# Two-layer hybrid trunk on one core: expert outputs placed back inside the next pair, gate folded into the hidden product, first norm and pool scale fed differently

## The chip, the cores and the metric
The kernel runs on one core of one Trainium2 chip. The metric is the device time of one execution in microseconds, as a median of several runs. The core has TensorE (PE in the profile), VectorE (DVE), ScalarE (ACT), GpSimd (POOL) and SyncE (SP); sixteen DMA engines fill its on-chip memory from HBM. PE writes its products to PSUM (eight banks of 512 fp32 columns on 128 partitions), from where DVE and ACT read them.

## What is computed
256 tokens of 2048 features go through two layers. Layer 0 mixes tokens by a causal trailing mean in four feature groups, layer 1 by stick-breaking attention on keys and values made from the stream; each is followed by a mixture of 16 experts, of which every token takes two of one group of four. The sizes: D = 2048, expert width F = 512.

```python
def pool_mixer(x, pool_w, pool_scale):          # four groups of 512 features, windows 2, 4, 8, 16
    ...
    y = jnp.einsum("bsgc,gcd->bsgd", pooled, pool_w).reshape(B, S, D)
    return y * pool_scale

def hier_moe(x, w_grp, b_grp, w_rt, b_rt, w_gate, w_up, w_down):
    ...                                          # gate: (T, 16), two entries of a row are not zero
    h = jax.nn.silu(jnp.einsum("td,edf->tef", xt, w_gate)) * jnp.einsum("td,edf->tef", xt, w_up)
    y = jnp.einsum("tef,efd->td", h * gate[:, :, None], w_down)
    return y.reshape(B, S, D)

def reference(...):
    for i in range(2):
        if i == 0: h = h + pool_mixer(rmsnorm(h, norm_mix[0]), ...)
        else:      h = h + stick_breaking_layer(rmsnorm(h, norm_mix[1]), k, v, ...)
        h = h + hier_moe(rmsnorm(h, norm_ffn[i]), ...)
```

## The kernel before
**Weights.** They are read once, in loads of 1 MiB issued by SP into a ring of 12 slots (`ring`). An expert takes 12 slots: four of gate and four of up, in turn (`m` = 0 to 7), and four of down (`m` = 8 to 11). A load into a slot waits until PE has read what is there (`slot_read`, L378 in the loop, L341 before it), so a wait of PE can hold back loads. The first five loads of expert 1 go to a buffer of their own (`extra`, L362).

**Experts.** `moe(l)` on each engine does the router and then 16 experts in 8 pairs; on PE pair 0 stands outside a hardware loop over the other seven. At most 64 tokens (CAP) of an expert are handled; a branch for more stands behind the loops and isn't taken here. For each expert `e` of a pair (`b` = 0, 1), PE does:
- gate and up (L1308): 32 fp32 products of `xg` (the gathered tokens, transposed) with four quarters of the weights; the gate half goes to partitions 0 to 63, the up half to 64 to 127. After each quarter two slots are free.
- the gather of the next expert (L1258 for its three parts of the norm factor `rs`, L1264 for 16 feature tiles, 96 small bf16 products with the 0/1 matrix `pick`)
- transposes: of `put`, 0/1 times the gate (L1318), and of `hid` (L1320)
- down (L1331): 16 fp32 products of `hidT` with the down weights, a slot free after each four.

ACT makes silu of the gate half with the scale `rs_slot` (L542) once all eight slots are read; DVE multiplies it with the up half to `hid` (L918); ACT copies `putT` and `hidT` (L545, L546), and PE waits for these ahead of down. ACT and DVE copy the outputs of down to `y_rows` (L551, L928), two quarters each. After both experts of a pair PE puts the rows back to their tokens: eight fp32 products of `putT` (128 x 256) with `y_rows` (L1341), each into a bank that DVE adds to the stream `resid` (L938); a product waits for the add but one before it.

**Router.** Ahead of the loop PE makes the logits, DVE picks the groups and experts in some 30 small steps (L815 to L894), PE counts slots, and `gather(0)` collects the tokens of expert 0. PE runs products of constants in between (`keep_clock`, L1229). DVE then scales the gathered tokens to `xg` (L904), first half and second half; the first gate product waits for the first half.

**Opening and pooling.** x and the band table are loaded by ACT's queue, the constants and norm vectors by SP's. PE transposes the vectors (L1387), DVE spreads them and makes the first norm (L801; POOL does the power, L449) and the scaled bands (L976); PE's band products (L1397, L1398) follow, ACT and DVE split them into two fp32r parts (L580, L983). The four groups of the pooling product run as units of 12 fp32r products (L1179), weights split by ACT (L501) and DVE (L764). The pool scale, a row in `vec_rows`, is spread over the partitions by PE (L1222, bank 7), copied by ACT to `mixed` (L589), multiplied on DVE with the product (L1003) and added to `resid` (L1007). The router's parts of the stream follow group by group on ACT, POOL (L456, L462) and DVE (L777, L783).

## Time and profile before

| | us |
|---|---|
| three runs | 1464.21, 1467.04, 1467.81 |
| median | 1467.04 |
| the profiled execution | 1467.67, of which the span from first to last instruction is 1465.8 |
| PE busy in the span | 1386.4 |
| expert loop of layer 0 on PE | about 87.9 to 555.8 |
| expert loop of layer 1 on PE | about 992.3 to 1461.5 |

The page gives busy time by engine; a view by windows gives for a stretch the busy time of each engine with the number of its instructions, the granted clock of PE (1.00 is 2.4 GHz, 0.50 is 1.2 GHz), the busy share of the DMA engines and what they moved; the timeline merges like instructions that follow each other (start, length, what, how many), with the idle time ahead of them and what ended it in brackets. PE shows two records for one fp32 product. Numbers with L are lines of the kernel.

### The profile page before, as it was taken

The page shows a single profiled execution, that of the slowest core. Times are in us where ns is not written, and L with a number is a line of the kernel's source. Part 1 is how long each engine was busy: PE and PEld are TensorE (multiplying, and loading weights), DVE is VectorE, ACT ScalarE, POOL GpSimd, SP SyncE. Part 2 cuts the span into 40 slices and gives each one's busy share as a digit, 9 for nine tenths or more (in the row PEclk, how much of TensorE's full clock was granted, in tenths as well). Part 3 has the DMA queues.
Part 4 walks back from the last instruction along what each step waited for, and adds up shares of the span by engine and source line. Part 5 has one row for each costly group of instructions (what it writes and reads, how often), then busy time and mean ns, then how long its engine had stood idle before and what let it go on. Part 6 is the DMA issues. An engine that isn't in the chain of part 4 may idle for free.

```text
span 1465.8 us, 22517 instructions
## 1 busy us (share of the span) xinstructions
PE 1386.4 (95%) x9100; PEld 767.0 (52%) x9100; DVE 530.1 (36%) x832; ACT 387.2 (26%) x585; POOL 40.3 (3%) x33
## 2 busy tenths in 40 slices
PE   6889999999999998999999998989999999999998
PEld 5653334334333436888888887764343343333433
DVE  3742121221221215656566665561213212212122
ACT  3621011000010115565656565440001001100010
POOL 0110000000000000100000000010000000000000
PEclk9989999999999998999999999999999999999999
DMA  9768899999999999554554543568799999999995
GB/s 327 323 253 351 363 422 422 422 422 422 422 422 422 422 411 326 173 181 164 162 175 150 172 156 132 176 248 337 291 422 421 422 422 421 422 422 422 422 422 231
DMA packets 95028, 480.62 MB, mean 328 GB/s; under 512 B 9218, under 2 KB 9316, under 8 KB 45572
## 3 DMA queue, kind: packets, MB, share of 16 engines
q1 hardware_dynamic: 94548, 477.07, 82.1%
q10 hardware_dynamic: 432, 2.88, 0.5%
q8 instruction: 34, 0.56, 0.1%
q14 instruction: 14, 0.11, 0.0%
HBM read 477.82 MB, written 2.10 MB: 327 GB/s over the span
## 4 chain that ended last, share of the span: by engine, by line
issue 53%; PE 39%; DVE 3%; ACT 3%; POOL 1%; DMA 1%; SPq 0%; POOLq 0%; ACTq 0%; DVEq 0%
PE ps L1308 15%; PE ps L1331 8%; PE ps L1179 6%; PE ps L1341 4%; PE ps L1264 3%; POOL head_rs L485 1%; DVE ws L764 1%; ACT parts L517 1%; DMA vec_rows<-in_q_norm 1%; ACT ws L501 1%; PE ps L1397 1%; PE ps L1320 0%; DVE rest L777 0%; ACT hidT L546 0%; ACT junk L514 0%
## 5 line engine op out<-in xcount | busy, mean ns | idle before, releaser
L1308 PE MATMUL ps<-ring,xg 128*64 128x512 f32 x1968 | 432.0, 593 | 0.6 <-issue 0.6
L1179 PE MATMUL ps<-ws,xs 128*128 128x512 f32 x1632 | 385.4, 395 | 7.0 <-DVE ws L764 2.8
L1179 PEld LDWEIGHTS ps<-ws,xs 128*128 128x128 f32 x1632 | 304.9, 189 | 75.5 <-DVE ws L764 5.3
L1308 PEld LDWEIGHTS ps<-ring,xg 128*64 128x64 f32 x1968 | 142.8, 137 | 279.2 <-issue 279.2
L1331 PE MATMUL ps<-ring,hidT 128*64 128x512 f32 x1024 | 226.8, 595 | 21.9 <-ACT hidT L546 21.9
L918 DVE SCALAR_TENSOR_TENSOR hid<-ps,rs_slot,silu_g 64x512 f32<-64x512 f32 x32 | 24.0, 752 | 433.0 <-ACT silu_g L542 433.0
L767 DVE SCALAR_TENSOR_TENSOR ws<-ring,vecs,ws 128x512 fp32r<-128x512 f32 x192 | 134.5, 748 | 92.0 <-ACT ws L504 92.0
L542 ACT ACTIVATE silu_g<-ps,rs_slot 64x512 f32<-64x512 f32 x32 | 21.8, 682 | 514.4 <-PE ps L1308 514.4
L1331 PEld LDWEIGHTS ps<-ring,hidT 128*64 128x64 f32 x1024 | 73.8, 137 | 151.2 <-issue 131.7
L504 ACT ACTIVATE ws<-ring,vecs 128x512 fp32r<-128x512 f32 x192 | 127.4, 715 | 94.2 <-PE ps L1179 86.1
L1341 PE MATMUL ps<-y_rows,putT 128*128 128x512 f32 x256 | 123.4, 618 | 12.1 <-ACT y_rows L551 12.0
L928 DVE COPY y_rows<-ps 64x512 f32<-64x512 f32 x64 | 41.6, 690 | 238.5 <-PE ps L1331 238.5
L1264 PE MATMUL ps<-pick,parts 128*128 128x64 bf16 x3264 | 102.2, 194 | 0.0
L938 DVE TENSOR_TENSOR resid<-resid,ps 128x512 f32<-128x512 f32 x128 | 87.9, 687 | 30.4 <-PE ps L1341 28.6
L1264 PEld LDWEIGHTS ps<-pick,parts 128*128 128x128 bf16 x3264 | 98.2, 98 | 0.5
L551 ACT ACTIVATE y_rows<-ps 64x512 f32<-64x512 f32 x64 | 34.3, 584 | 231.3 <-PE ps L1331 231.3
L1341 PEld LDWEIGHTS ps<-y_rows,putT 128*128 128x128 f32 x256 | 39.8, 188 | 96.6 <-DVE resid L938 58.0
L764 DVE TENSOR_TENSOR ws<-ring,ws 128x1024 fp32r<-128x1024 f32 x40 | 50.5, 1267 | 51.9 <-ACT ws L501 51.9
L904 DVE TENSOR_TENSOR xg<-ps,ffn_gain 128x512 f32<-128x512 f32 x68 | 46.4, 682 | 24.0 <-PE ps L1264 24.0
L501 ACT ACTIVATE ws<-ring 128x1024 fp32r<-128x1024 f32 x40 | 41.5, 1053 | 46.6 <-PE ps L1179 38.8
L545 ACT ACTIVATE putT<-ps 128x128 f32<-128x128 f32 x32 | 8.9, 277 | 88.7 <-PE ps L1320 88.7
L485 POOL TENSOR_TENSOR head_rs<-head_ssq,half 128x8 f32<-128x8 f32 x8 | 16.7, 2082 | 251.1 <-DVE head_ssq L1029 251.1
(153 smaller groups left out, 640.2 us busy)
## 6 DMA issues: line engine op xcount, KB each, us to landing
ring<-in_moe_w_down SPq DMA_DIRECT2D x128, 1024.0 KB, 15.5
ring<-in_moe_w_up SPq DMA_DIRECT2D x124, 1024.0 KB, 15.0
ring<-in_moe_w_gate SPq DMA_DIRECT2D x122, 1024.0 KB, 13.2
ring<-in_w_kv SPq DMA_DIRECT2D x32, 1024.0 KB, 5.5
ring<-in_w_q SPq DMA_DIRECT2D x16, 1024.0 KB, 5.0
ring<-in_w_o SPq DMA_DIRECT2D x16, 1024.0 KB, 5.0
extra<-in_moe_w_gate SPq DMA_DIRECT2D x6, 1024.0 KB, 7.8
ring<-in_pool_w SPq DMA_DIRECT2D x4, 1024.0 KB, 15.4
```

Source lines behind the costliest of these rows:

```text
L501: nc.scalar.activation(dst, four(n)[:, 2 * h:2 * h + 2, :], ACT.Copy).then_inc(unit_hi, 1)
L504: last = nc.scalar.activation(dst[:, k, :], four(n)[:, 2 * h + k, :], ACT.Copy, scale=vecs[:, gain + k:gain + k + 1])
L764: nc.vector.tensor_tensor(ws[:, b, 1], src, ws[:, b, 0].bitcast(F32), ALU.subtract).then_inc(unit_lo, 1)
L767: last = nc.vector.scalar_tensor_tensor(out=ws[:, b, 1, k, :], in0=src[:, k, :], scalar=vecs[:, gain + k:gain + k + 1], in1=ws[:, b, 0, k, ...
L904: nc.vector.tensor_tensor(xg[:, b, 8 * h:8 * h + 8, :], ps[:, 6 + h, :].rearrange("p (k s) -> p k s", k=8), per_feature(ffn_gain[:, l, 8 * ...
L928: nc.vector.tensor_copy(y_rows[CAP * b:CAP * b + CAP, (2 * h + 1) * BLK:(2 * h + 2) * BLK], ps[CAP:2 * CAP, 2 + h, :]).then_inc(y_dve, 1)
L938: nc.vector.tensor_tensor(rb, rb, ps[:, 4 + t, :], ALU.add).then_inc(resid_added, 1)
L1179: last = mm(ps[:, bank + t, :], xs[:, px, k, cols], ws[:, b, pw, j, :], start=(first and j == 0 and n == 0), stop=(last_unit and j == 1 an ...
L1264: last = mm(ps[:, 6 + k // 8, (k % 8) * CAP:(k % 8 + 1) * CAP], parts[:, s, t, k * P:(k + 1) * P], pick[:, t, e, :], start=(s == 0 and t = ...
L1308: last = mm(ps[CAP * h:CAP * h + CAP, b, :], xg[:, b, k, :], both[h][:, j, :], start=(k == 0), stop=(k == KD - 1))
L1331: last = mm(ps[CAP * h:CAP * h + CAP, 2 + c // 2, :], hidT[:, b, k, :], down[:, c * BLK:(c + 1) * BLK], start=(k == 0), stop=(k == KF - 1))
L1341: mm(ps[:, 4 + t, :], putT[:, t * P:(t + 1) * P], y_rows[:, c * BLK:(c + 1) * BLK], start=True, stop=True).then_inc(mix_done, 1)
```

## The change
**Experts.** The gate is no longer in the matrix that puts the rows back but in the silu-up product: `gate` times `rs` is split into three bf16 parts (`gate_parts`, five DVE steps ahead of the loop), which are gathered with those of `rs` in one product of six columns (`side`, `make_side`); DVE sums both (`slot_scale`), ACT uses the first for silu, DVE the second for `hid`. `put` and its making go; PE makes `putT` from `pick` itself, by two bf16 products with the identity, once per pair. The outputs of down are taken by ACT alone, rounded to fp32r (`y_hi`), and DVE subtracts that from the output in PSUM to get the rest (`y_lo`, eight operations a pair). Putting back is 16 fp32r products a pair, and they stand in the next pair, two outputs after each quarter of its first gate and up step; those of the last pair stand behind the loop. DVE's adds of a pair move to the head of the next pair, ahead of `hid`. The gather is split: 11 of 16 tiles stand ahead of the transposes, the rest behind them, ahead of the wait for `hidT`. For expert 0 the scales are gathered after the tokens, not before.

**Opening and pooling.** The constants are loaded after the norm vectors; the pool scale is spread by DMA with broadcast (groups 0 and 1 by SP ahead of the router's rows and the second pooling weight, groups 2 and 3 by POOL once the buffer's former rows are used) to `scale_row`; PE's spreading and ACT's copies go. DVE multiplies the product in PSUM in place and adds from there; PE may use the bank again after the add, not after the multiplication. The first mean square stands ahead of DVE's wait for the transposed vectors. PE's products of constants at the start number 56 pairs of 128 columns instead of 9 of 256, need only a memset, and stand ahead of the wait for the tables; those of the router (24 and 10) have the same columns as before, in halves.

```diff
+gate_parts = at(26 * KB + 512, "gate_parts", [P, NT, EXP + 2, 3], BF16)
...
+y_lo012 = at(96 * KB, "y_lo012", [P, 3, BLK], F32R)
+y_lo = [y_lo012[:, 0, :], y_lo012[:, 1, :], y_lo012[:, 2, :], y_lo3[:, :]]
 member = at(27 * KB + 512, "member", [P, NT, EXP], BF16)
...
-WARM_START, WARM_ROUTE, WARM_PICK = 9, 24, 10
+WARM_START, WARM_ROUTE, WARM_PICK = 56, 24, 10
+TURN_AT = 11
...
-    sp.dma_start(const[:], table).then_inc(table_loaded, 16)
...
     sp.dma_start(vec_rows[V_HEAD + 1:V_END, :], q_norm).then_inc(band_loaded, 16)
-    sp.dma_start(vec_rows[V_SCALE:V_ROWS, :], pool_scale.rearrange("a (k p) -> (a k) p", p=P)).then_inc(table_loaded, 16)
+    sp.dma_start(const[:], table).then_inc(table_loaded, 16)
     load(0, pool_w_v[0])
...
+    for g in range(2):
+        sp.dma_start(scale_row[:, g, :], pool_scale[:, g * BLK:(g + 1) * BLK].to_broadcast([P, BLK])).then_inc(scale_loaded[g], 16)
...
+    for g in range(2, NG):
+        pool.wait_ge(mixed_done, 2 * (g - 2) + 2)
+        pool.dma_start(scale_row[:, g % 2, :], pool_scale[:, g * BLK:(g + 1) * BLK].to_broadcast([P, BLK])).then_inc(scale_loaded[g], 16)
...
                 act.wait_ge(slot_read, n0 + SLOTS * (2 * i + b) + 8)
                 nc.scalar.activation(silu_g[:, :], ps[0:CAP, b, :], ACT.Silu,
-                                     scale=rs_slot[:, b:b + 1]).then_inc(silu_done, 1)
+                                     scale=slot_scale[:, b, 0:1]).then_inc(silu_done, 1)
                 act.wait_ge(hid_turned, EXP * l + 2 * i + b + 1)
-                nc.scalar.activation(putT[:, b * P:(b + 1) * P], ps[:, 1 - b, SEQ:SEQ + P], ACT.Copy)
                 nc.scalar.activation(hidT[:, b], ps[:, 1 - b, 0:KF * CAP].rearrange("p (k s) -> p k s", k=KF),
                                      ACT.Copy).then_inc(hidT_done, 1)
+                if b == 0:
+                    nc.scalar.activation(putT[:, :], ps[:, 1, SEQ:2 * SEQ], ACT.Copy).then_inc(putT_done, 1)
...
+                for c in range(NBLK):
+                    h = c % 2
+                    nc.scalar.activation(y_hi[CAP * b:CAP * b + CAP, c, :],
+                                         ps[CAP * h:CAP * h + CAP, 2 + c // 2, :],
+                                         ACT.Copy).then_inc(y_hi_done, 1)
...
-        act.wait_ge(scale_spread, g + 1)
-        if g:
-            act.wait_ge(resid_added, 2 * g)
-        nc.scalar.activation(mixed[:, :, :], ps[:, 7, :].unsqueeze(1).to_broadcast([P, NT, BLK]),
-                             ACT.Copy).then_inc(scale_out, 1)
...
+        step(nc.vector.tensor_tensor(rs_parts[:, :, 2], rs_rest[:, :], rs_parts[:, :, 1], ALU.subtract))
+        nc.vector.tensor_copy(side[:, :, 0, 0:3], rs_parts[:, :, :])
+        nc.vector.tensor_copy(side[:, :, 1, 0:3], rs_parts[:, :, :])
...
-        def make_put(i):
-            dve.wait_ge(pick_done, (NPAIR + 1) * l + i + 1)
-            nc.vector.tensor_tensor(put[:, :, :, :], pick[:, :, :, :],
-                                    gate[:, :, bass.ds(2 * i, 2)].unsqueeze(3).to_broadcast([P, NT, 2, CAP]),
-                                    ALU.mult).then_inc(put_done, 1)
+        def make_side(i):
+            nc.vector.tensor_copy(side[:, :, :, 3:6], gate_parts[:, :, bass.ds(2 * i, 2), :]).then_inc(side_done, 1)
...
+        step(nc.vector.tensor_tensor(gate_rs[:, :, :], gate[:, :, 0:EXP],
+                                     rs[:, :].unsqueeze(2).to_broadcast([P, NT, EXP]), ALU.mult))
+        step(nc.vector.tensor_copy(gate_parts[:, :, 0:EXP, 0], gate_rs[:, :, :]))
+        step(nc.vector.tensor_tensor(gate_rest[:, :, :], gate_rs[:, :, :], gate_parts[:, :, 0:EXP, 0], ALU.subtract))
+        step(nc.vector.tensor_copy(gate_parts[:, :, 0:EXP, 1], gate_rest[:, :, :]))
+        step(nc.vector.tensor_tensor(gate_parts[:, :, 0:EXP, 2], gate_rest[:, :, :], gate_parts[:, :, 0:EXP, 1],
+                                     ALU.subtract))
+        make_side(0)
...
         tokens_out(G0 + 1, 0)
-        make_put(0)
...
-            dve.wait_ge(hid_turned, EXP * l + 2 * i + 2)
-            make_put(i + 1)
...
+        def add_rows(i):
             for m in range(8):
                 c, t = m // 2, m % 2
                 dve.wait_ge(mix_done, 8 * NPAIR * l + 8 * i + m + 1)
                 rb = resid[:, t, c * BLK:(c + 1) * BLK]
                 nc.vector.tensor_tensor(rb, rb, ps[:, 4 + t, :], ALU.add).then_inc(resid_added, 1)
+        def pair(i, before=None):
+            if before is not None:
+                add_rows(before)
+            for b in range(2):
+                dve.wait_ge(silu_done, EXP * l + 2 * i + b + 1)
+                nc.vector.scalar_tensor_tensor(out=hid[:, :], in0=ps[CAP:2 * CAP, b, :],
+                                               scalar=slot_scale[:, b, 1:2], in1=silu_g[:, :],
+                                               op0=ALU.mult, op1=ALU.mult).then_inc(hid_done, 1)
+                tokens_out(G0 + 2 * i + 2 + b, 1 - b)
+                if b == 0:
+                    dve.wait_ge(hid_turned, EXP * l + 2 * i + 1)
+                    make_pick(i + 1)
+                    make_side(i + 1)
+                for c in range(NBLK):
+                    h = c % 2
+                    dve.wait_ge(y_hi_done, NBLK * (EXP * l + 2 * i + b) + c + 1)
+                    nc.vector.tensor_tensor(y_lo[c][CAP * b:CAP * b + CAP, :], ps[CAP * h:CAP * h + CAP, 2 + c // 2, :],
+                                            y_hi[CAP * b:CAP * b + CAP, c, :].bitcast(F32),
+                                            ALU.subtract).then_inc(y_lo_done, 1)
+        pair(0)
+        with dve.Fori(1, NPAIR) as i:
+            pair(i, i - 1)
+        add_rows(NPAIR - 1)
...
+    nc.vector.memset(counters[:, 1, :], 1.0).then_inc(ones_done, 1)
+    mean_square(0, True)
     dve.wait_ge(vec_turned, 1)
...
     nc.vector.tensor_copy(counters[:, 0, :], tri)
-    nc.vector.tensor_copy(ident_b[:, :], ident)
-    nc.vector.tensor_copy(counters[:, 1, :], ones).then_inc(vec_done, 1)
-    mean_square(0, True)
+    nc.vector.tensor_copy(ident_b[:, :], ident).then_inc(vec_done, 1)
...
-                dve.wait_ge(scale_out, g + 1)
+                dve.wait_ge(scale_loaded[g], 16)
...
-            nc.vector.tensor_tensor(mixed[:, t, :], ps[:, MIX_BANKS[g % 2] + t, :], mixed[:, t, :],
-                                    ALU.mult).then_inc(mixed_done, 1)
+            mixed = ps[:, MIX_BANKS[g % 2] + t, :]
+            nc.vector.tensor_tensor(mixed, mixed, scale_row[:, g % 2, :], ALU.mult).then_inc(mixed_done, 1)
             rb = resid[:, t, g * BLK:(g + 1) * BLK]
             dve.wait_ge(mixed_done, 2 * g + t + 1)
-            nc.vector.tensor_tensor(rb, rb, mixed[:, t, :], ALU.add).then_inc(resid_added, 1)
+            nc.vector.tensor_tensor(rb, rb, mixed, ALU.add).then_inc(resid_added, 1)
...
-    def spread_scale(g):
-        if g:
-            pe.wait_ge(scale_out, g)
-        for k in range(4):
-            row = V_SCALE + 4 * g + k
-            last = mm(ps[:, 7, k * P:(k + 1) * P], const[0:V_ROWS, row:row + 1].to_broadcast([V_ROWS, P]),
...
-        last.then_inc(scale_spread, 1)
...
-            mm(ps[:, 3, 0:2 * P], counters[:, 0, :], counters[:, :, :].rearrange("p a b -> p (a b)"),
-               start=True, stop=True)
+            for c in (0, P):
+                mm(ps[:, 3, c:c + P], counters[:, 1, :], counters[:, 1, :], start=True, stop=True)
...
-                last = mm(ps[0:CAP, e, 508:511], pick[:, t, e, :], rs_parts[:, t, :], start=(t == 0),
+                last = mm(ps[0:CAP, e, 506:512], pick[:, t, e, :], side[:, t, e, :], start=(t == 0),
                           stop=(t == NT - 1))
...
+        def gather(e, tiles):
+            for k in tiles:
...
-        pe.wait_ge(rs_parts_done, l + 1)
         pe.wait_ge(pick_done, PICKS + 1)
-        gather(0)
+        gather(0, range(KD))
+        pe.wait_ge(side_done, PICKS + 1)
+        gather_scales(0)
...
+        def put_rows(i, m):
...
+            c, t = m // 2, m % 2
+            if t == 0:
+                pe.wait_ge(y_lo_done, NBLK * (EXP * l + 2 * i + 1) + c + 1)
+            pe.wait_ge(resid_added, add0 + 8 * i + m - 1)
+            mm(ps[:, 4 + t, :], putT[:, t * P:(t + 1) * P], y_hi[:, c, :], start=True, stop=False)
+            mm(ps[:, 4 + t, :], putT[:, t * P:(t + 1) * P], y_lo[c], start=False, stop=True).then_inc(mix_done, 1)
+        def pair(i, before=None):
             for b in range(2):
                 pe.wait_ge(xg_done, 2 * (XG + 2 * i + b) + 1)
                 pe.wait_ge(hidT_done, (EXP + 1) * l + 2 * i + b + 1)
+                if b == 1:
+                    pe.wait_ge(putT_done, NPAIR * l + i + 1)
                 for q in range(4):
                     both = [loaded(i, b, 2 * q + h).rearrange("p (k c) -> p k c", k=4) for h in range(2)]
                     if q == 2:
...
                     last.then_inc(slot_read, 2)
+                    if b == 0 and before is not None:
+                        put_rows(before, 2 * q)
+                        put_rows(before, 2 * q + 1)
...
-                pe.wait_ge(rs_slot_done, XG + 2 * i + b + 2)
-                pe.wait_ge(put_done, PICKS + i + 1)
+                    pe.wait_ge(side_done, PICKS + i + 2)
+                gather_scales(1 - b)
+                gather(1 - b, range(TURN_AT))
+                pe.wait_ge(slot_scale_done, XG + 2 * i + b + 2)
                 pe.wait_ge(hid_done, EXP * l + 2 * i + b + 1)
-                nc.tensor.transpose(ps[:, 1 - b, SEQ:SEQ + P], put[:, b].rearrange("p e s -> p (e s)"), ident)
+                if b == 0:
+                    for t in range(NT):
+                        mm(ps[:, 1, SEQ + t * P:SEQ + (t + 1) * P], pick[:, t].rearrange("p e s -> p (e s)"),
+                           ident_b[:, :], start=True, stop=True)
+                else:
+                    gather(0, range(TURN_AT, TURN_AT + 1))
                 for k in range(KF):
                     last = nc.tensor.transpose(ps[:, 1 - b, k * CAP:(k + 1) * CAP], hid[:, k * P:(k + 1) * P],
                                                const[0:CAP, C_ID:C_ID + CAP])
                 last.then_inc(hid_turned, 1)
+                gather(1 - b, range(TURN_AT + b, KD))
                 pe.wait_ge(hidT_done, (EXP + 1) * l + 2 * i + b + 2)
                 if b == 1:
-                    pe.wait_ge(y_act, 2 * (EXP * l + 2 * i) + 2)
-                    pe.wait_ge(y_dve, 2 * (EXP * l + 2 * i) + 2)
+                    pe.wait_ge(y_lo_done, NBLK * (EXP * l + 2 * i + 1))
...
-            for m in range(8):
-                c, t = m // 2, m % 2
-                if t == 0:
-                    pe.wait_ge((y_act, y_dve)[c % 2], 2 * (EXP * l + 2 * i) + 3 + c // 2)
-                pe.wait_ge(resid_added, add0 + 8 * i + m - 1)
-                mm(ps[:, 4 + t, :], putT[:, t * P:(t + 1) * P], y_rows[:, c * BLK:(c + 1) * BLK],
-                   start=True, stop=True).then_inc(mix_done, 1)
...
         pair(0)
         with pe.Fori(1, NPAIR) as i:
-            pair(i)
+            pair(i, i - 1)
+        for m in range(8):
+            put_rows(NPAIR - 1, m)
...
+    pe.wait_ge(ones_done, 1)
+    keep_clock(WARM_START)
     pe.wait_ge(table_loaded, TABLES)
     pe.wait_ge(band_loaded, 32)
     nc.tensor.transpose(ps[:, 4, 0:V_END], vec_rows[0:V_END, :], const[0:V_END, C_ID:C_ID + V_END]).then_inc(vec_turned, 1)
-    pe.wait_ge(vec_done, 1)
-    keep_clock(WARM_START)
...
-                pe.wait_ge(mixed_done, 2 * (g - 2) + t + 1)
+                pe.wait_ge(resid_added, 2 * (g - 2) + t + 1)
         unit(2 * g, (4 * g, 4 * g + 1), True, False, read, bank=MIX_BANKS[g % 2])
-        spread_scale(g)
         unit(2 * g + 1, (4 * g + 2, 4 * g + 3), False, True, bank=MIX_BANKS[g % 2])
```

## Rows read from the trace of the kernel before

**Rows 1.** The page: busy time, share of the span, instructions of each engine
```profile
PE 1386.4 (95%) x9100; PEld 767.0 (52%) x9100; DVE 530.1 (36%) x832; ACT 387.2 (26%) x585; POOL 40.3 (3%) x33
```

**Rows 2.** View by windows: one pair of experts in layer 0 (columns above)
```profile
199.68:258.34 58.66, 56.61 (x416) 22.93 (x414) 13.42 (x23) 5.89 (x11) 0.00 (x0) 1.00 1.01 422
```

**Rows 3.** Timeline of PE: one pair of layer 0, and the start of the next
```profile
204.87 13.95 PE L1308 MATMUL ps<-ring,xg 128*64 128x512 f32 x64
...
218.79 2.97 PE L1264 MATMUL ps<-pick,parts 128*128 128x64 bf16 x96
221.60 0.31 PE L1318 MATMUL ps<-const,put 128*128 128x128 f32 x1
...
222.94 7.09 PE L1331 MATMUL ps<-ring,hidT 128*64 128x512 f32 x32 [0.64 <-ACT hidT L546]
...
255.72 7.70 PE L1341 MATMUL ps<-y_rows,putT 128*128 128x512 f32 x16 [0.77 <-ACT y_rows L551]
263.34 1.94 PE L1308 MATMUL ps<-ring,xg 128*64 128x512 f32 x8
```

**Rows 4.** Tile ring: landing times, loads issued 208.6 to 267.0, then 442.5 to 500.9
```profile
DMA to landing us min/median/max: 7.3/13.5/18.8
...
DMA to landing us min/median/max: 12.1/18.3/23.6
```

**Rows 5.** PE timeline and ring landings: expert 15 of layer 0, then of layer 1
```profile
522.19 13.90 PE L1308 MATMUL ps<-ring,xg 128*64 128x512 f32 x64
...
L378 SPq DMA_DIRECT2D ring<-in_moe_w_up x1: 333/333/333, 511.8 to 511.8; - x1
...
DMA to landing us min/median/max: 19.9/19.9/19.9
...
1427.80 13.90 PE L1308 MATMUL ps<-ring,xg 128*64 128x512 f32 x64
...
L378 SPq DMA_DIRECT2D ring<-in_moe_w_up x1: 333/333/333, 1417.5 to 1417.5; - x1
...
DMA to landing us min/median/max: 18.8/18.8/18.8
```

**Rows 6.** View by windows: pair 0 and the start of pair 1
```profile
120.00:160.00 40.00, 38.63 (x247) 14.96 (x244) 9.41 (x15) 3.59 (x6) 0.00 (x0) 1.00 0.79 302
```

**Rows 7.** Chain by time: 48 fp32r products; the page's group of DVE's adds
```profile
857.12 10.91 PE ps L1179 x48
...
L938 DVE TENSOR_TENSOR resid<-resid,ps 128x512 f32<-128x512 f32 x128 | 87.9, 687 | 30.4 <-PE ps L1341 28.6
```

**Rows 8.** Tile ring: two loads issued one after the other, and their landings
```profile
L341 SPq DMA_DIRECT2D ring<-in_moe_w_down x1: 328/328/328, 137.9 to 137.9; - x1
...
DMA to landing us min/median/max: 8.0/8.0/8.0
...
L341 SPq DMA_DIRECT2D ring<-in_moe_w_gate x1: 327/327/327, 150.1 to 150.1; - x1
...
DMA to landing us min/median/max: 4.7/4.7/4.7
```

**Rows 9.** Timeline: the gates of layer 0 are made, and the first expert product
```profile
85.88 0.18 DVE L894 TENSOR_TENSOR gate<-route 128x32 f32<-128x32 f32 x1
...
87.85 5.37 PE L1308 MATMUL ps<-ring,xg 128*64 128x512 f32 x24 [0.41 <-issue]
```

**Rows 10.** Timeline of the pooling stage: a spread scale on PE, DVE in group 3
```profile
44.38 1.05 PE L1222 MATMUL ps<-vec_rows,const 98*128 98x128 f32 x8
...
66.40 0.69 DVE L1003 TENSOR_TENSOR mixed<-ps,mixed 128x512 f32<-128x512 f32 x1 [0.74 <-ACT mixed L589]
```

**Rows 11.** Timeline of the opening: the scaled bands, and the first pooling unit
```profile
15.04 1.15 DVE L976 TENSOR_SCALAR band_s<-band,rs 128x1024 f32<-128x1024 f32 x2 [0.89 <-POOL rs L449]
...
32.56 5.49 PE L1179 MATMUL ps<-ws,xs 128*128 128x512 f32 x12
```

**Rows 12.** View by windows: PE waits for DVE ahead of the router
```profile
65.00:75.00 10.00, 3.21 (x20) 1.98 (x24) 8.46 (x13) 7.51 (x15) 3.69 (x3) 0.70 0.74 306
```

73 lines of the change are left out of this document (25 added, 48 removed).

## The prediction, made before the changed kernel was run

> **What bounds the kernel now.** I read the page first, then the stretches of the expert loops, then the landings of the weight loads. The page says 95% busy for PE [rows 1], which invites the conclusion that every matmul removed is time gained. The view by windows corrects it: over one pair of experts PE is busy 56.6 of 58.66 us, but in the same stretch the DMA engines are at 1.01 of their share and move 422 GB/s [rows 2]. A pair of experts needs 24 loads of 1 MiB, 25.17 MB, and 25.17 MB at 422 GB/s is 59.6 us. PE takes a pair in 58.47 us (from the first matmul of one pair at 204.87 to that of the next at 263.34 [rows 3]). So PE already consumes faster than the queue delivers, and lives on a lead. The landings show that lead melting: the shortest time from issue to landing within a pair is 7.3 us for the pair issued from 208.7 and 12.1 us four pairs later [rows 4], 1.2 us more in each pair; 58.47 + 1.2 = 59.67 us, the same number by another road. One load therefore lands every 2.486 us (59.67 / 24). No matmul of the loop waits for a load in this trace, but the lead is nearly used up when a layer ends. In the last pair of layer 0 the last up block of expert 15 is issued at 511.8 and lands 19.9 us later, at 531.7; PE started that expert at 522.19 and came to that block (last quarter of 13.8 us) at 532.5. The lead is 0.8 us. In layer 1 the same block lands at 1417.5 + 18.8 = 1436.3, and PE came to it at 1427.80 + 10.3 = 1438.1, 1.8 us of lead [rows 5].
>
> What remains to be gained in a layer is then: the lead, the time in which the queue stood idle before it became continuous, and what follows the last load. The queue stood idle around pair 0: 302 GB/s over 120 to 160 us is 302/422, so 11.4 us of 40 were lost; after that it never stops [rows 2, 6].
>
> **The change part by part: the loop.** Of the 58.47 us [rows 3]: the eight fp32 put products and the wait for ACT in front of them, from 254.95 (255.72 less 0.77) to 263.34, are 8.39. They become 16 fp32r products. 48 fp32r products of the same 128x512 shape took 10.91 us, 0.227 each [rows 7], so 16 cost 3.64. Two waits of 0.64 for hidT go: the left-over gather tiles (5 of 16, a fraction of the 2.81 us from 218.79 to 221.60, so 0.9 us) cover the copy, and if that cover fails each expert pays the 0.64 again. The two fp32 transposes of put (0.3 each) become two bf16 products, some 0.12 together by the pace of the gather. PE's new need per pair: 58.47 - 8.39 + 3.64 - 1.28 - 0.6 + 0.12 = 52.0 us. New waits: the put products stand on PE between the quarters of the next gate and up step and wait for y_lo and for the adds; behind them stand the next quarter and, through it, the freeing of slots. The first is due 3.4 us after the pair before ends, y_lo of that block is ready after about 1.4 us (an ACT copy and one subtraction), each next one 0.7 later, and one quarter brings DVE only two adds, so none of these waits bites. DVE loses four copies and gains eight subtractions of some 0.69 [rows 7] a pair, 13.4 to about 16 of 59 us [rows 2]; that is hidden. The order on DVE (adds of the old pair first, then hid) could hold the transposes by under 1 us; hidden as well, as follows.
>
> 52.0 us is under the 59.67 us that the queue needs. **From pair 1 on the loop becomes DMA-bound**, with PE waiting some 7.7 us a pair for loads, in pieces of at most about 1.5 us (a quarter of the gate and up step takes 3.44 us and its two loads arrive in 4.97). So almost all of the 6.5 us saved in a pair is not gained. What is gained is worked out for each layer.
>
> *The gap of the queue.* The last down load of expert 2 is issued at 137.9 and lands 8.0 us later, at 145.9; the next one (expert 3) waits until the first quarter of pair 1 has been read, issue 150.1, landing 4.7 us later, at 154.8 [rows 8]. Between the two issues lie the 8.39 us of the put. With the put gone from there, and the two experts of pair 0 shorter by some 0.9 us each, that issue comes at about 140, and its landing is limited by the one before it: that one was late too and comes at about 143.6, so 143.6 + 2.5 = 146.1. Gain 8.7 us of the 11.4. From there each load is 2.486 us behind the one before, to the end of the layer, so the last load moves by the same 8.7 us. The same gap stands in layer 1.
> *After the last gate and up load.* PE now reaches it exactly when it lands: the lead of 0.8 us (layer 0) and 1.8 us (layer 1) is gained. Then the hidT wait and the put transpose are gone: 0.9 us.
> *The tail of a layer.* The last pair's put has no next pair to hide in. After the last down product ACT copies (0.6), DVE subtracts four times and then adds eight times, 12 x 0.69 = 8.3 us on one engine [rows 7]; before, 8.39 + 0.69. I take 0.4 us gained.
>
> **The router stage in front of each loop.** gather(0) moves ahead and now ends before its scales, while DVE must make five more steps (gate times rs, and its three parts) after the gates at 85.88, and copy them, before the scales can be gathered, reduced and xg scaled. One such step is 0.2 us. Gates at 86.1 plus 0.35 (two more copies and one more wait before slot_of) plus 5 x 0.2 plus 0.2 gives 87.7; scales 0.2, reduction 0.25, first half of xg 0.7, so PE starts at 88.9 instead of 87.85 [rows 9]. Cost 1.1 us in each layer, and it is fully paid, since the queue is waiting for PE to free slots there.
>
> **Pooling stage.** The four spreads of the pool scale (eight PE records each, 1.05 us [rows 10]) and ACT's four copies of them go; the product is made in PSUM, at the same DVE price. Two of the spreads lie on the chain that leads PE, ACT, DVE to the mixed rows of group 1: twice 1.05 less a little overlap with the units' products, 1.75 us. In group 3 DVE also waited 0.74 us for ACT's copy [rows 10]. Together 2.5 us. The two loads that POOL issues instead wait for the mixed rows of groups 0 and 1 and stand ahead of its first subtraction, for which DVE and ACT have other work; their data are due two groups later, some 10 us. No row shows a DMA issued by POOL; the bounds are nothing, and two of POOL's mean operations (40.3/33 = 1.2 us [rows 1]), 2.4 us, if none of it is covered. POOL is 3% busy, so I take nothing.
>
> **Opening.** DVE's first norm no longer stands behind the vector copies: POOL's inverse root, for which DVE waited 0.89 us before 15.04, comes earlier; band_s is ready about 1.1 us sooner [rows 11]. Against it: 0.5 MB of broadcast scale now lies ahead of the second pool_w load (1.2 us at 422 GB/s, up to double for short rows), on which ACT's copies and so the xs parts depend, and PE, warmed before the vectors arrive, then idles until band_s is there, so that the first band products may run at 1.2 GHz (a unit of 12 products took 5.49 us at that level against 2.75 [rows 11]). No row shows how these mix; bounds -1 (gain) to +3, I take +0.7.
>
> **Sum** against the profiled execution (span 1465.8, time 1467.67): opening and pooling +0.7 - 2.5 = -1.8. Layer 0: +1.1 - 8.7 - 0.8 - 0.9 - 0.4 = -9.7. Layer 1: +1.1 - 8.7 - 1.8 - 0.9 - 0.4 = -10.7. Total -22.2, so 1445.5 us; this run stands 0.6 us above the median of the three, 1467.04, so **1445 us**.
>
> A page of the Trainium skill, "DMA: Bandwidth & Descriptors" (section Specifications), names a ceiling of 435 GB/s for the core's 16 DMA engines, 3% over what this queue does. By that rule a load would land every 2.41 us, and the sum, an estimate from that page, would come to about 1422 us. The trace does not show it: with landings 12 to 24 us after their issue [rows 4], so a full queue, the rate stays at 422 [rows 2]. The same section gives 358 GB/s as the limit of HBM per core; this trace is 18% above that, so the measurement decides.
>
> **Rivals.** (1) *The queue has speed in reserve.* The rate seen is then only what PE asked for. For it: PE never waits for a load now. Against it: the time to landing grows from pair to pair, which a queue with reserve would not show [rows 4]. If it were so, PE's 52.0 us a pair would set the time at the far end: some 41 us a layer, 1467 - 83 - 1 = about 1383 us. Short of that, about 155 loads a layer follow the gap, so each percent of reserve is 155 x 0.025 = 3.9 us a layer; 3% give 1422 us. Chance 0.05 for all of it. The ceiling that the page names would be this rival's case of 3%. (2) *The gap is not refilled*, because something else holds the first loads of pair 1: then only leads, transposes, tails, pooling remain, 22.2 - 17.4 = 4.8, so 1462 us. Chance 0.05. (3) *The opening costs its upper bound*: +2.3 on my value, and POOL's 2.4, so 1450 us. Chance 0.10. (4) *Slower: the clock falls in the loop.* PE now waits in every quarter. In this trace the granted clock fell after PE had done nothing from 65 to 70 us, and 65 to 75 shows 0.70 on average [rows 12]. A stretch of s us at 1.2 GHz costs PE s/2. PE has 7.7 us a pair to spare and the change 22 us over 15 pairs to lose, so it turns slower from (7.7 + 1.5) x 2 = 18 us at 1.2 GHz in each pair. At 25 us in each pair: (12.5 - 7.7) x 15 = 72, so 1445 + 72 = 1517 us. Against it: the longest new wait is 1.5 us, and the loops now, with waits of 0.8 us, are granted 1.00 throughout [rows 2]. Chance 0.04.
>
> **How the numbers follow.** My forecast has 0.72, its own range 1440 to 1450 (the bounds of the opening and of POOL, and 0.2% for the rate, worth 1 us per layer); the rivals 0.05, 0.05, 0.10, 0.04; 0.04 is left for what I do not see. The range of 8 in 10 takes in the forecast and rival 3: 1438 to 1453. A measurement of this kernel tells about 0.3% (4.4 us) from no change, so faster is below 1462.6: 0.91 (forecast, rivals 1 and 3, half of 2, and part of the rest), same 0.05, slower 0.04.
>
> **What would show it right or wrong.** In the loop of the changed kernel: a period of 59.6 to 59.7 us, longer than now; 422 GB/s; PE waits ahead of the gate and up products, released by loads of ring, some 7 us a pair; the wait ahead of the down products gone. The window 120 to 160 near 400 GB/s. The first expert product about 0.7 us earlier in layer 0. It is wrong if the period follows PE's 52 us, if the clock shows 0.5 in the loops, or if a new wait ahead of the transposes exceeds what the loads leave.

## The result and the profile after

The changed kernel takes **1447.94 us** (median of 4 runs, 1446.9 to 1450.29) against 1465.96 us of the kernel before beside it: ratio 0.988, 95% interval 0.986 to 0.990. The forecast was 1445. The profiled run is the longest of the four: 1450.29 us, span 1448.4, against 1467.67 and 1465.8; the step by step account below is between these two, 17.4 us.

View by windows of the changed kernel (columns as in [rows 2]): a pair in which PE still has loads in hand, a pair in which it has none, pair 0 to 1, and two stretches that are discussed below.
```profile
203.60:263.30 59.70, 59.70 (x481) 26.06 (x481) 18.13 (x31) 9.10 (x15) 0.00 (x0) 1.00 1.01 422
382.60:442.30 59.70, 54.70 (x424) 23.51 (x419) 15.46 (x26) 8.47 (x15) 0.00 (x0) 1.00 1.01 422
120.00:160.00 40.00, 40.00 (x354) 18.32 (x350) 12.71 (x22) 6.05 (x10) 0.00 (x0) 1.00 0.96 389
541.00:547.50 6.50, 5.39 (x11) 3.27 (x12) 4.30 (x8) 0.00 (x0) 0.00 (x0) 0.50 1.05 386
886.00:889.00 3.00, 3.00 (x8) 2.33 (x8) 0.71 (x1) 0.00 (x0) 0.00 (x0) 0.50 0.03 10
```
The queue runs at the same 422 GB/s as before [rows 2]. What changed is at its two ends: 389 instead of 302 GB/s around pair 0 [rows 6], that is 3.1 instead of 11.4 us of 40 lost, and later in the layer PE waits for loads. The page's busy times (to set against [rows 1]), its group of gate and up products, and the landing times of the loads issued from 442.5 to 501 (to set against [rows 4]):
```profile
PE 1358.4 (94%) x9239; PEld 775.5 (54%) x9239; DVE 567.1 (39%) x910; ACT 423.4 (29%) x629; POOL 41.3 (3%) x35
...
L1337 PE MATMUL ps<-ring,xg 128*64 128x512 f32 x1968 | 447.1, 596 | 45.4 <-DMA ring<-in_moe_w_up 43.0
...
DMA to landing us min/median/max: 21.8/23.7/25.5
```
Timeline of PE: two starts of a pair with loads in hand and the last down step between them, the first wait for a load, an expert later in the layer, then the last expert of layer 0 (compare [rows 3, 5]).
```profile
189.49 3.60 PE L1337 MATMUL ps<-ring,xg 128*64 128x512 f32 x16
...
236.13 7.09 PE L1369 MATMUL ps<-ring,hidT 128*64 128x512 f32 x32
...
243.04 3.60 PE L1337 MATMUL ps<-ring,xg 128*64 128x512 f32 x16
...
280.14 3.65 PE L1337 MATMUL ps<-ring,xg 128*64 128x512 f32 x16 [0.66 <-DMA ring<-in_moe_w_up]
...
449.40 3.60 PE L1337 MATMUL ps<-ring,xg 128*64 128x512 f32 x16
453.99 3.65 PE L1337 MATMUL ps<-ring,xg 128*64 128x512 f32 x16 [0.99 <-DMA ring<-in_moe_w_up]
459.06 3.65 PE L1337 MATMUL ps<-ring,xg 128*64 128x512 f32 x16 [1.42 <-DMA ring<-in_moe_w_up]
463.94 3.65 PE L1337 MATMUL ps<-ring,xg 128*64 128x512 f32 x16 [1.22 <-DMA ring<-in_moe_w_up]
...
523.61 3.65 PE L1337 MATMUL ps<-ring,xg 128*64 128x512 f32 x16 [1.22 <-DMA ring<-in_moe_w_up]
...
530.60 7.09 PE L1369 MATMUL ps<-ring,hidT 128*64 128x512 f32 x32
```
PE's own pace is 243.04 - 189.49 = 53.55 us a pair; the queue's is 59.67 (the load that lands at 147.7 and the one that lands at 523.4 are 151 loads apart, 2.49 us for each). PE catches up with the queue at 280, in pair 3, and from there waits in every step of gate and up, down to the last: the last up load of layer 0 lands at 523.4 and PE goes on at 523.61.

The same points in both profiled runs, in us from the start. The third column is the shift so far, the fourth what this step adds, the fifth what the prediction had for it.

| point | before | after | shift | step | predicted |
|---|---|---|---|---|---|
| first extra load issued (end of pooling) | 63.53 | 61.94 | -1.6 | -1.6 | -1.8 |
| first expert product, layer 0 | 87.85 | 87.36 | -0.5 | +1.1 | +1.1 |
| last up load lands | 531.7 | 523.4 | -8.3 | -7.8 | -8.7 |
| last down step begins | 540.20 | 530.60 | -9.6 | -1.3 | -1.7 |
| last add ends | 556.47 | 548.78 | -7.7 | +1.9 | -0.4 |
| first attention product | 569.61 | 559.01 | -10.6 | -2.9 | 0 |
| first load freed at layer 1's router | 902.10 | 892.61 | -9.5 | +1.1 | 0 |
| first load freed by layer 1's experts | 999.81 | 991.21 | -8.6 | +0.9 | +1.1 |
| last up load lands | 1436.3 | 1419.6 | -16.7 | -8.1 | -8.7 |
| last down step begins | 1446.01 | 1426.67 | -19.3 | -2.6 | -2.7 |
| last add ends | 1462.27 | 1444.14 | -18.1 | +1.2 | -0.4 |
| end of the span | 1465.8 | 1448.4 | -17.4 | +0.7 | 0 |

Each column is one execution, and some of these steps differ by 1 to 3 us between executions of the same code; where the other profiles show that, it is said below.

### The profile page after: what moved, and what is told of

Its sections match the earlier page's. It is cut to its first block, busy times and chain, and to the rows that moved or that the text cites. A ratio compares the mean times of both kernels' runs of the same rounds, so it can differ in the third digit from the quotient of the medians.

```text
span 1448.4 us, 22975 instructions
## 1 busy us (share of the span) xinstructions
PE 1358.4 (94%) x9239; PEld 775.5 (54%) x9239; DVE 567.1 (39%) x910; ACT 423.4 (29%) x629; POOL 41.3 (3%) x35
## 4 chain that ended last, share of the span: by engine, by line
issue 53%; PE 24%; DMA 16%; DVE 3%; ACT 2%; POOL 1%; SPq 0%; POOLq 0%; DVEq 0%; ACTq 0%
DMA ring<-in_moe_w_up 16%; PE ps L1337 9%; PE ps L1204 6%; PE ps L1369 3%; PE ps L1281 2%; POOL head_rs L496 1%; PE ps L1319 1%; DVE ws L772 1%; DMA const<-in_constant_table 1%; PE ps L1428 1%; ACT parts L528 1%; ACT ws L512 1%; PE ps L1320 1%; DVE rest L785 0%; ACT junk L525 0%
## 5 line engine op out<-in xcount | busy, mean ns | idle before, releaser
L1337 PE MATMUL ps<-ring,xg 128*64 128x512 f32 x1968 | 447.1, 596 | 45.4 <-DMA ring<-in_moe_w_up 43.0
L956 DVE TENSOR_TENSOR y_lo<-ps,y_hi 64x512 fp32r<-64x512 f32 x128 | 88.2, 689 | 218.9 <-ACT y_hi L564 215.9
L553 ACT ACTIVATE silu_g<-ps,slot_scale 64x512 f32<-64x512 f32 x32 | 21.8, 683 | 460.7 <-PE ps L1337 460.7
L564 ACT ACTIVATE y_hi<-ps 64x512 fp32r<-64x512 f32 x128 | 75.7, 591 | 239.2 <-PE ps L1369 236.8
L944 DVE SCALAR_TENSOR_TENSOR hid<-ps,slot_scale,silu_g 64x512 f32<-64x512 f32 x32 | 24.1, 752 | 242.8 <-ACT silu_g L553 242.4
L1281 PE MATMUL ps<-pick,parts 128*128 128x64 bf16 x3264 | 107.8, 194 | 0.8 <-DVE pick L878 0.8
L1319 PE MATMUL ps<-y_hi,putT 128*128 128x512 f32 x128 | 59.6, 465 | 6.5 <-DVE resid L936 3.5
L1319 PEld LDWEIGHTS ps<-y_hi,putT 128*128 128x128 f32 x128 | 24.9, 195 | 61.4 <-issue 48.2
L1320 PE MATMUL ps<-y_lo,putT 128*128 128x512 f32 x128 | 52.7, 412 | 0.0
L556 ACT ACTIVATE hidT<-ps 128x256 f32<-128x256 f32 x32 | 12.3, 384 | 78.3 <-PE ps L1358 78.3
```

Of the source, the lines that this page charges most:

```text
L564: nc.scalar.activation(y_hi[CAP * b:CAP * b + CAP, c, :], ps[CAP * h:CAP * h + CAP, 2 + c // 2, :], ACT.Copy).then_inc(y_hi_done, 1)
L956: nc.vector.tensor_tensor(y_lo[c][CAP * b:CAP * b + CAP, :], ps[CAP * h:CAP * h + CAP, 2 + c // 2, :], y_hi[CAP * b:CAP * b + CAP, c, :].b ...
L1281: last = mm(ps[:, 6 + k // 8, (k % 8) * CAP:(k % 8 + 1) * CAP], parts[:, s, t, k * P:(k + 1) * P], pick[:, t, e, :], start=(s == 0 and t = ...
L1319: mm(ps[:, 4 + t, :], putT[:, t * P:(t + 1) * P], y_hi[:, c, :], start=True, stop=False)
L1320: mm(ps[:, 4 + t, :], putT[:, t * P:(t + 1) * P], y_lo[c], start=False, stop=True).then_inc(mix_done, 1)
L1337: last = mm(ps[CAP * h:CAP * h + CAP, b, :], xg[:, b, k, :], both[h][:, j, :], start=(k == 0), stop=(k == KD - 1))
```

## The experiments

**Was it the queue's gap?** First the part that has nothing to do with the experts is taken back, then the place of the put.

*e1: old opening and pooling.* The edit takes back every part of the change ahead of the router:
```
-            pe.wait_ge(ones_done, 1)
-            keep_clock(WARM_START)
             pe.wait_ge(table_loaded, TABLES)
...
+            pe.wait_ge(vec_done, 1)
+            keep_clock(WARM_START)
...
                 unit(2 * g, (4 * g, 4 * g + 1), True, False, read, bank=MIX_BANKS[g % 2])
+                spread_scale(g)
```


> The changed kernel with its opening and pooling part put back as it was before the change (order of the first norm, spread of the pool scale by PE and ACT, nine warming products behind the vectors); the experts' part stays new. Theory: opening and pooling brought the 1.6 us by which the extra loads at the end of pooling are issued earlier in the changed kernel, and what is gained there is kept to the end: 1447.9 + 1.6 = 1449.5 us. Rival: that gain is lost again later (the half-clock stretch of 3.4 us at the end of the attention stage, which only the changed kernel has, comes from it): 1447.9 or a little less, and that stretch is gone.

Measured: 1453.1 us, ratio 0.991 (0.989 to 0.993). That is 3.6 us over the expectation. In its profile the first extra load is issued at 63.7 us, 1.8 later than in the profiled run of the changed kernel, and the span is 2.8 longer. But that run is at the edge here: in nine profiles with the changed kernel's opening and pooling (its own, that of e12, which is the same kernel again, and those of the versions e2 to e6, e8 and e9 below, which leave this part as it is) the load is issued between 59.6 and 61.9 us, 60.7 in the middle one; with the old part it is 63.5, 63.7 and 63.7 (the kernel before, e7, which is a version of it, and e1). First the changed kernel as profiled, then e3:
```profile
L369 SPq DMA_DIRECT2D extra<-in_moe_w_gate x3: 327/431/433, 61.9 to 74.8; - x3
...
L369 SPq DMA_DIRECT2D extra<-in_moe_w_gate x3: 328/432/433, 59.6 to 72.5; - x3
```
So opening and pooling bring 1.6 to 4.1 us at their own place, 3.0 in the middle. All four runs of this kernel (1451.5 to 1453.7) are slower than all four of the changed one, by 5.2 us in the medians; where the other 2 us go isn't shown. The rival falls: the half-clock stretch near 886 is there too, from 890 on.

*e2: the put at the end of its own pair.*
```
-                            if b == 0 and before is not None:
-                                put_rows(before, 2 * q)
-                                put_rows(before, 2 * q + 1)
...
                             last.then_inc(slot_read, 1)
+                    for m in range(8):
+                        put_rows(i, m)
```


> The changed kernel, but the put products of a pair stand at its own end again (still two fp32r passes), and so do the adds. PE then waits 1.4 us for the first y_lo and is held by DVE's four subtractions and eight adds: some 8.2 us between the last down product of a pair and the next pair's first product, instead of 4.5 us of put inside the next pair. PE's pair is 53.55 - 4.5 + 8.2 = 57.3 us, below the queue's 59.67. Theory (what was gained is the gap of the queue at pair 0 and 1): the gap comes back, 7.7 to 8.2 us in each layer, 1447.9 + 16 = 1464 us, within 3. Rival (the fp32r put gave the gain by being short on PE, wherever it stands): 1448 to 1450. Second rival (PE's pace counts, 3.7 us more in each of 16 pairs): 1448 + 60 = 1508.

Measured: 1464.4 us, ratio 0.9985 (0.9975 to 0.9994): nearly everything that the change brought is gone. Windows and timeline of this kernel:
```profile
120.00:160.00 40.00, 36.65 (x305) 16.79 (x301) 11.60 (x19) 5.39 (x8) 0.00 (x0) 0.96 0.79 309
...
203.60:263.30 59.70, 56.41 (x424) 24.59 (x422) 15.56 (x26) 8.42 (x14) 0.00 (x0) 0.97 1.01 422
...
529.08 3.65 PE L1335 MATMUL ps<-ring,xg 128*64 128x512 f32 x16 [1.09 <-DMA ring<-in_moe_w_up]
```
309 GB/s around pair 0, as before the change, and the last quarter of expert 15 still waits 1.09 us for its load: the queue sets the end of the layer, and the queue is late by its gap. Halving the put's passes brought nothing where it stood; from the last down product of a pair to the next pair's first product it takes 9.5 us (250.07 to 259.59), or 8.8 in a pair that keeps the full clock (192.63 to 201.38), against 8.4 before [rows 3]. At the end of six of layer 0's eight pairs the granted clock falls to 0.50 for some us, after PE stood still twice for 1.4 to 1.8 us; at the end of the other two it stays at 1.00 after waits of 1.5 and 1.6 us; this is the only kernel here in which rival 4, a fall within the loop, is seen.

**How much does PE have to spare?** The prediction said 7.7 us in each pair. Products were added to PE behind the down step of the first expert of pairs 1 to 7 (n of them, 8 in e3 and 24 in e4):
```
+                            if b == 0 and k == KF - 1 and before is not None:
+                                pe.wait_ge(resid_added, add0 + 8 * before + 8)
+                                for _ in range(n):
+                                    last = mm(ps[0:CAP, 4, :], hidT[:, b, k, :], down[:, 0:BLK], start=True, stop=True)
```


> The changed kernel with 8 more fp32 products of 128x512 behind the down step of the first expert of pairs 1 to 7 (written to a bank that is free then, used by nobody). A product of this shape takes 13.9/64 = 0.217 us, so PE gets 1.74 us more in a pair, 12.2 us in a layer. PE waited for loads 43.0 us in the two layers of the changed kernel, 21.5 us in each. Theory (account of a layer: nothing is lost until the added work is over 21.5 us): 1447.9 to 1449.5. Rival (PE sets the time): + 14 x 1.74 = 24 us, 1472.

> The same with 24 products: 5.2 us more in a pair, PE's pair 58.8 us, still under the 59.67 us of the queue; 36.5 us in a layer. Account of a layer: 36.5 - 21.5 = 15 us lost in each, 1448 + 30 = 1478, within 5, since PE begins pair 1 behind the queue and must catch up with it. Account by the pair, as the prediction had it (7.7 us to spare in each pair, every pair for itself): 1448 to 1450. PE sets the time from the first product on: + 73, 1521.

Measured: 1488.2 us (+40.2) and 1681.7 us (+233.8). All expectations missed, since the added products cost four times what I had put down for them. Starts of pairs in the kernel with 8, then in that with 24, and 24 added products in a row (each leaves two records; one is missing):
```profile
314.94 3.60 PE L1337 MATMUL ps<-ring,xg 128*64 128x512 f32 x16
...
375.36 3.60 PE L1337 MATMUL ps<-ring,xg 128*64 128x512 f32 x16
...
283.48 3.60 PE L1337 MATMUL ps<-ring,xg 128*64 128x512 f32 x16
...
312.89 20.33 PE L1374 MATMUL ps<-ring,hidT 128*64 128x512 f32 x47
...
357.67 3.60 PE L1337 MATMUL ps<-ring,xg 128*64 128x512 f32 x16
```
A pair takes 60.42 and 74.19 us instead of 53.55: 6.87 and 20.64 more, 0.86 for each product. With the right price the two runs decide after all. By the pair, 60.42 is only 0.75 over the queue's 59.67, so 14 pairs should lose 10.5 us; 40.2 were lost. By the layer, 7 x 6.87 = 48.1 us were added and 20.1 lost, and 144.5 added and 116.9 lost: 28.0 and 27.6 us were free. The timeline of the changed kernel gives nearly that: at its own pace PE would have begun the last down step at 236.13 + 5 x 53.55 = 503.9 us, and it began at 530.60, 26.7 us later. (The 43.0 us of the page, 21.5 a layer, are less; the starts count the wait in full, while the idle time is taken from a matmul's modelled end.) So PE has 28/7 = 4.0 us a pair to spare, not 7.7: in pairs 1 and 2 it is not waiting but catching up.

*e5: 4 products.* The account of the layer is put to a test that it could fail:

> The changed kernel with 4 added fp32 products behind the down step of the first expert of pairs 1 to 7. Alone in its place such a product took 0.86 us in the runs with 8 and 24 of them (PE's pair 60.42 and 74.19 us against 53.55 unhindered), not the 0.217 us that I had divided out of a step in which products for two halves of the array run side by side. So 3.44 us a pair, 24.1 us in a layer; PE's pair 57.0 us. Account of a layer, mended by those two runs (they lost 40.2 and 233.8 us for 96.2 and 289 us of added work, so about 28 us of a layer are free, which is 6.12 us of waiting in each of the last 4.65 pairs): 24.1 is under 28, so 1447.9 to 1449.5 us. Rival (PE's pace sets the time): + 48, 1496.

Measured: 1450.5 us (1449.2 to 1453.5), ratio 0.990 (0.988 to 0.992). PE got 48 us more to do, and the time rose by some 2, 1 more than the account had at most and far from the rival's 1496; the waits for loads shrink from 43.0 to 5.1 us on the page:
```profile
L1337 PE MATMUL ps<-ring,xg 128*64 128x512 f32 x1968 | 453.3, 595 | 7.3 <-DMA ring<-in_moe_w_up 5.1
```

**Who sets the pace, before and after?** The down loads are made half as large, in both kernels (e6 the changed one, e7 the one before). The down products read the loaded half twice, so the second half of the down result is left out:
```
-                return w_down_v[l, e, :, m - 8, :]
+                return w_down_v[l, e, :, m - 8, 0:2 * BLK]
...
-                                          down[:, c * BLK:(c + 1) * BLK], start=(k == 0), stop=(k == KF - 1))
+                                          down[:, h * BLK:(h + 1) * BLK], start=(k == 0), stop=(k == KF - 1))
```


> The changed kernel with down loads of half the size: of each block of w_down only the first 1024 columns are loaded, and the down products read those twice, as many products of the same shape as before (the second half of the down result is left wrong). A pair's 24 loads shrink from 25.17 to 20.97 MB, 49.7 us at 422 GB/s, below PE's 53.55. Theory (the loops follow the queue): all waits for loads go, 28 us a layer, 1448 - 56 = 1392 us, within 4. Rival (the queue doesn't bind, PE does): 1448.

> The same halving of the down loads in the kernel before the change. Its PE waits for no load anywhere in the loops, and its pair is 58.47 us with or without the smaller loads. Theory: before the change PE set the time, and the queue was only about to: 1466 to 1467.5 us, no change. Rival (the loops followed the queue before the change as well): some 5 to 8 us a layer less, 1450 to 1457.

Measured: after, 1395.1 us, ratio 0.951 (0.949 to 0.953), 53 us less; before, 1464.8 us beside 1465.0, ratio 0.999 (0.998 to 1.000). The page's group of gate and up products and a window of the changed kernel with small loads, then the window of the kernel before with them:
```profile
L1337 PE MATMUL ps<-ring,xg 128*64 128x512 f32 x1968 | 440.5, 594 | 1.8 <-DVE xg L919 1.8
...
203.60:263.30 59.70, 59.70 (x504) 26.62 (x500) 18.26 (x31) 9.11 (x15) 0.00 (x0) 1.00 0.98 397
...
203.60:263.30 59.70, 57.65 (x418) 23.22 (x416) 14.13 (x24) 5.89 (x11) 0.00 (x0) 1.00 0.87 353
```
No wait for a load is left in the changed kernel, and PE is busy throughout the window. One edit, worth 53 us to one kernel and at most 3 to the other. Before the change PE set the time, with its last loads landing 0.8 and 1.8 us before it came to them; after it the queue does, by 26.5 us a layer here and 28 by e3 and e4. While the queue sets the pace, a faster put or gather inside the loop would only lengthen PE's waits.

**What the misses were worth.** Three steps of the table stand out: the router (+1.1 and +0.9, as predicted), the tails (+1.9 and +1.2 instead of -0.4) and the opening, where band_s should have come 1.1 us sooner. Each gets a version that does away with it.

*e8: the first expert's tokens ahead of the gates.* Timeline of the changed kernel (compare [rows 9]):
```profile
83.12 2.96 PE L1281 MATMUL ps<-pick,parts 128*128 128x64 bf16 x96 [0.48 <-DVE pick L878]
...
84.68 0.18 DVE L900 TENSOR_TENSOR gate<-route 128x32 f32<-128x32 f32 x1
...
86.05 0.18 DVE L883 COPY side<-gate_parts 128x12 bf16<-128x12 bf16 x1
...
86.63 1.27 DVE L919 TENSOR_TENSOR xg<-ps,ffn_gain 128x512 f32<-128x512 f32 x2
```
The first half of the tokens is gathered by about 84.6, but xg stands on DVE behind the gates, their three parts and the scales, none of which it needs.
```
+                half_out(G0 + 1, 0, 0)
                 step(nc.vector.tensor_tensor(SCORE[:, :, 1:5, :], HOT1[:, :, 1:5, :], HOT2[:, :, 1:5, :], ALU.add))
...
+                half_out(G0 + 1, 0, 1)
...
+                            if b == 0 and before is None and q == 2:
+                                pe.wait_ge(side_done, PICKS + 1)
+                                gather_scales(0, 1)
```


> The changed kernel with the start of a layer's first expert taken out from behind the gates: its tokens are scaled as soon as they are gathered; the gates, the parts of the root and the gathered scales come after, beside the first gate and up products; PE's warming products ahead of the gather are 6 pairs instead of 10. Theory (the prediction's router term, 1.1 us a layer, is fully paid, as is everything on the path to the first gate and up product): the slots come free earlier, so both layers move: selection 0.6 us earlier, scaling about 2.0 us earlier, 2.6 us a layer, 1447.9 - 5.2 = 1442.7, within 2. Rival (the end of a layer hangs on a queue that doesn't see the start): 1448.

Measured: 1443.0 us, ratio 0.984 (0.982 to 0.986). From the first extra load to the first expert product it takes 23.5 instead of 25.4 us, and in layer 1, from the first load freed at the router to the first expert product, 2.1 to 2.8 us less (88.3 against 91.1, and 90.5 in e12). Timeline of this kernel:
```profile
81.46 0.69 DVE L887 TENSOR_TENSOR xg<-ps,ffn_gain 128x512 f32<-128x512 f32 x1 [0.18 <-PE ps L1292]
...
82.86 0.69 DVE L887 TENSOR_TENSOR xg<-ps,ffn_gain 128x512 f32<-128x512 f32 x1 [0.38 <-PE ps L1292]
83.16 7.09 PE L1346 MATMUL ps<-ring,xg 128*64 128x512 f32 x32 [0.41 <-issue]
```
These 4.1 to 4.7 us are about what the time fell by (from 1447.9 or, in e12, 1448.3, to 1443.0): the start of a layer is paid in full, through the slots that it frees.

*e9: the tail.* Timeline of the changed kernel, end of layer 0:
```profile
538.35 2.85 DVE L956 TENSOR_TENSOR y_lo<-ps,y_hi 64x512 fp32r<-64x512 f32 x4 [6.96 <-ACT y_hi L564]
539.09 0.50 PE L1319 MATMUL ps<-y_hi,putT 128*128 128x512 f32 x1 [1.41 <-DVE y_lo L956]
...
541.23 1.28 DVE L936 TENSOR_TENSOR resid<-resid,ps 128x512 f32<-128x512 f32 x2
542.07 0.77 PE L1319 MATMUL ps<-y_hi,putT 128*128 128x512 f32 x1 [1.76 <-DVE resid L936]
542.63 0.63 PE L1320 MATMUL ps<-y_lo,putT 128*128 128x512 f32 x1
```
PE stands 1.41 and 1.76 us, the granted clock falls to 0.50 in 541 to 547.5 (the window above; before the change PE was at 1.00 there), a product takes 0.63 instead of 0.40, and DVE, which was to be the bound, waits for PE. How much of the tail is due to the clock can be read from e2, where the same subtractions, put products and adds follow each other at the end of every pair, and in some pairs the clock stays up. A window over one of these, DVE's subtractions and its last two adds there:
```profile
192.45:202.10 9.65, 6.06 (x22) 2.81 (x22) 7.90 (x12) 3.65 (x5) 0.00 (x0) 1.00 1.01 421
...
193.29 2.85 DVE L954 TENSOR_TENSOR y_lo<-ps,y_hi 64x512 fp32r<-64x512 f32 x4 [6.96 <-ACT y_hi L564]
...
200.73 1.29 DVE L936 TENSOR_TENSOR resid<-resid,ps 128x512 f32<-128x512 f32 x2 [0.23 <-PE ps L1318]
```
From the last down product (192.63) to the last add (202.02) that is 9.4 us at full clock, against 9.2 before the change. The ten profiles that have this tail show it twenty times: 10.3 to 10.5 us long where the mean granted clock in it is 0.83 or 0.84, and 10.8 to 11.3 us where it is 0.69 to 0.76. So the half clock costs 0.9 to 1.9 us a tail, and the chain alone 0.2.
```
+                        if c < 2:
...
+                        else:
+                            mm(ps[:, bank, :], mine.bitcast(F32), y_full[:, c - 2, :], start=True, stop=True)
```


> The changed kernel with the last pair of each layer written out by itself. For its last two column blocks ACT keeps the whole fp32 value and PE makes one fp32 put product of it; only the first two blocks take the split in two and the two fp32r passes; the second block's products have banks of their own; eight pairs of warming products stand on PE while it waits. DVE's serial chain is 2 + 8 operations of 0.69 us instead of 4 + 8. The tail (last down product to last add) took 10.4 us in the changed kernel and 9.2 before. Theory (the tail is DVE's serial chain plus the first copy, and the prediction's gain of 0.4 there was a loss of 1.2): 0.6 + 0.85 + 0.69 x 8 + some waiting = 8.2 us, 2.2 us a layer, 1447.9 - 4.4 = 1443.5, within 2. Rival (the tail's length is set by the half clock that falls on it; four fp32 products at 1.2 GHz take 7.7 us): 1447 to 1450.

Measured: 1442.2 us, ratio 0.984 (0.982 to 0.986), a little more than forecast. Its window over the tail of layer 0, and DVE there:
```profile
535.50:543.80 8.30, 7.04 (x34) 3.75 (x32) 6.49 (x10) 2.37 (x4) 0.00 (x0) 1.00 1.05 387
...
537.92 3.80 DVE L945 TENSOR_TENSOR resid<-resid,ps 128x512 f32<-128x512 f32 x6
```
From the last down product to the last add it takes 8.1 us in both layers, at full clock. The edit does two things at once. Two subtractions fewer are worth 2 x 0.69 = 1.4 us, and 9.4 - 1.4 = 8.0 us is what it takes at full clock; the other 0.9 to 1.9 us come from the clock, so the rival named a real cause. Whether the shorter wait or the warming products kept the clock up isn't settled.

*e10: the band first.*
```
+            dve.wait_ge(rs_done, 1)
+            dve.wait_ge(band_loaded, 32)
+            for t, (lo, hi) in enumerate(((0, 2), (2, 3))):
+                nc.vector.tensor_scalar(band_s[:, :, lo:hi, :], band[:, :, lo:hi, :], rs[:, t:t + 1], None,
+                                        ALU.mult).then_inc(band_done, 1)
             dve.wait_ge(vec_turned, 1)
```


> The changed kernel with another order in the opening: DVE scales the band as soon as the root is there (root at 12.03 us, band scaled from 14.71 in the changed kernel, behind the vectors and the tables), PE begins the band products then and turns the vectors after the second of them, and ACT copies the xs tiles before it comes to the second pool_w load. Theory (the first norm was moved ahead, but its user was not, so the prediction's gain of 1.1 us there stayed behind the constant table that now lands last): first band product at 13.3 instead of 16.0 us, the extra loads at the end of pooling issued 2 to 2.7 us earlier, 1447.9 - 2.4 = 1445.5, within 1.5. Rival (the landing of pool_w, not PE, sets the pooling stage): 1448.

Measured: 1446.7 us, ratio 0.986 (0.985 to 0.988), beside 0.987 for e12: 1.6 us in the medians where 2.4 were expected, too little to be told from nothing. Nor do the profiles show it: the first extra load is issued at 59.4 us, band_s begins at 13.45, and in the nine profiles with this part unchanged they come at 59.6 to 61.9 and at 13.28 to 14.80. DVE in the changed kernel and in this one:
```profile
14.71 1.14 DVE L1001 TENSOR_SCALAR band_s<-band,rs 128x1024 f32<-128x1024 f32 x2
...
13.45 1.15 DVE L996 TENSOR_SCALAR band_s<-band,rs 128x1024 f32<-128x1024 f32 x2 [2.37 <-DMA vec_rows<-in_q_norm]
```
What holds the band now is a small load, the row of q_norm, which shares the band's semaphore. In the changed kernel's profile the root was there at 12.03 us and the band was scaled only from 14.71, with nothing to use the root in between.

*e11 and e12: all three edits together, and the changed kernel beside them.*

> The three edits together: the first expert's tokens ahead of the gates, the tail by halves, the band first. Theory: they lie one behind the other on one path, so their gains add: 1443.0 - 4.4 - 2.4 = 1436.2, within 3. Rival (they shift work against the windows of the half clock, or the queue's gap grows by what the start gains): 1440 to 1443.

> The changed kernel as it is, on the same chip as the three before it, to set them against: 1447.9 us, 0.988 of the kernel before.

Measured: 1438.0 us, ratio **0.980** (0.979 to 0.982), against 1448.3 us, 0.987 (0.986 to 0.989). This version beats both kernels. The three gains, taken singly from 1448.3, are 5.3, 6.1 and 1.6 us; together they give 10.3 instead of 13.0. The expectation, 1436.2 within 3, holds, and runs of one kernel lie up to 5 us apart here, so a loss in adding them isn't shown.

## Why the prediction was right, point by point

**The bound.** Right. The 59.67 us of a pair's 24 loads are what a pair now takes from the point where PE has caught up, and e6 against e7 shows that the bound passed from PE to the queue. The reading behind it, a lead that melts by 1.2 us a pair [rows 4] under a queue that never stops [rows 2], is what made this forecast possible with 95% busy for PE on the page [rows 1].

**The rate, rival 1.** The queue has no reserve: PE waited for loads for 27 us a layer, and the rate stayed at 422 GB/s, as before. The Trainium skill, page "DMA: Bandwidth & Descriptors", section Specifications, gives a ceiling of 435 GB/s and an HBM limit of 358 per core. This queue of 1 MiB loads stays 3% under the first and 18% over the second, before and after the change, so the second didn't bind it.

**The gap.** Right in kind (e2), 0.6 to 0.9 us too large a layer. The load that was issued at 150.1 [rows 8] now is at 139.5, as forecast (140), but lands 8.2 us later at 147.7, not at 146.1. The term had the whole shift of the issue; 3.1 of the 11.4 us stay lost.

**After the last load.** 1.3 and 2.6 us against 1.7 and 2.7: right.

**PE's new pair.** 53.55 us, not 52.0. In pair 0, which has no put inside, the two experts take 24.34 and 24.18 us by their starts, 48.52 together; so the 16 put passes add 5.0 us to a pair, not 3.64. The 0.227 us of [rows 7] is the pace of 48 in one go, and in groups of four between other products a group costs 1.26 us, 0.31 for each. The experts took 58.47 - 8.39 = 50.08 us before, so they saved 1.6 us a pair, not 1.76. It changed nothing in the time, for the loops wait anyway; it is the slack, not the time, that was mis-sized.

**The spare time of rival 4.** Wrong, and an error of reasoning. "PE has 7.7 us a pair to spare" counts the difference of two periods in every pair. PE enters pair 1 behind the queue and must first catch up, so the spare time belongs to the layer: 27 to 28 us over 7 pairs (e3 to e5). The same rival's point on the clock holds: with waits of 1.4 us in each step the loops stay at 1.00.

**The router.** +1.1 and +0.9 against +1.1, five steps of 0.2 us: right, and paid in full (e8).

**The tails.** The step that failed: "DVE subtracts four times and then adds eight times, 12 x 0.69 = 8.3 us on one engine", 0.4 gained. The twelve operations do take that (8.1 to 8.2 us), and by the prediction's own numbers the gain was 0.2: 8.39 + 0.69 = 9.1 before, 0.6 + 8.3 = 8.9 after. The step left out two things. The adds wait for PE, three times 0.23 us, since each put product needs the bank of the add but one before it; that makes 9.4 us at full clock (e2). And PE, which stands still for 1.4 and 1.8 us here, drops to half clock, which the prediction had considered for the loop (rival 4) and not for the tail; that adds 0.9 to 1.9 us. In the two profiles of the table the tails are 1.9 and 1.2 us longer instead of 0.4 shorter, together 3.9 us on the wrong side, most of the 4.8 us that the sum missed (22.2 against 17.4).

**Opening and pooling.** -1.6 against -1.8 in the table, but the agreement is luck: the nine profiles of this part give 1.6 to 4.1 us, 3.0 in the middle, and the profiled run of the changed kernel is the one with the least. The parts (the spreads, the copies, the first norm) were not measured singly. The constant table now lands last (PE waits 4.2 us for it, to 13.53), and band_s comes at 14.71 instead of 15.04, 0.3 sooner and not 1.1; in the nine profiles it comes at 13.28 to 14.80.

**What I didn't see.** In the table attention begins 2.9 us earlier than the tail explains, and 1.1 us are lost later. Neither comes from the change. The profile of e7, whose code for these stages is that of the kernel before, has both as the changed kernel has them; PE from the end of its layer 0 on, and its window over the later stretch:
```profile
561.37 6.08 PE L1434 MATMUL ps<-const,resid 128*128 128x128 f32 x32 [5.45 <-issue]
567.21 3.03 PE L1179 MATMUL ps<-ws,xs 128*128 128x512 f32 x12
...
893.00:897.00 4.00, 3.22 (x8) 2.57 (x9) 1.86 (x2) 0.41 (x1) 0.00 (x0) 0.62 0.22 83
```
From the last add to the first attention product it takes 10.6 us there, 10.2 in the changed kernel and 13.1 in the profile before, where PE is at half clock until 570 and not 566. From there to the router's first load it takes 333.4 to 333.6 us in the eight profiles that show a half-clock stretch of some 3 to 4 us in that stage (e7, the changed kernel twice, and five of its versions) and 332.0 to 332.5 in the six that don't (the kernel before and five versions of the changed one). So 1.8 us of the table's 17.4 are a matter of which executions were profiled, and that the forecast came within 3 us of the median owes something to luck: the tails were 3.9 us worse than the sum had them, opening and pooling about 1.2 better.

## What to carry over

When an engine is at 95% and a queue at 1.01 of its share, work out both periods and then how far ahead of the queue the engine starts: what removed work brings is bounded by the gap in the queue, the lead at its end and what follows the last load. From the first expert product to the last down step both layers together gained 19.8 us, of the 79 (16 pairs of 4.92) by which PE's work became shorter. Spare time under a queue is a sum over the whole loop, beginning with the catching up, not a figure for each turn. And a piece of work that hides well inside the next turn of a loop has no next turn in the last one: cost that tail as a chain of its own, with the waits between its engines and with the clock of the engine that idles in it. Before a step of 1 or 2 us is read from two profiles, see how far it differs between executions of the same code.

## What the runs showed of the hardware

A 64-column fp32 product of 128x512 takes 0.434 us (13.9/32) where successive ones go to the two halves of the array in turn, and 0.86 us where all go to one half: 1.98 times. The page "TensorEngine Tiling (Array Packing)" of the Trainium skill, section Theoretical Speedup, gives up to 2 times for 64 columns, and the runs agree. I had taken the paired pace for products that go to one half only, and had divided it by the 64 records of 32 products, so that e3 and e4 became four times as heavy as meant.

Waits of 0.3 to 1.4 us in front of 3.65 us of products left the granted clock at 1.00 from 280 to 524 us, and in layer 1 as well. A wait of 1.4 us, 1.2 us of put products and a wait of 1.8 us stood ahead of a fall to 0.50 in each of the 18 tails of this form outside e2. In e2 nearly the same (1.5, 1.2 and 1.6 us) was followed by a fall at the end of some pairs and by none at the end of others, so these lengths alone don't decide it.
